# The mLSTM's values formed by feature in three jobs and turned by TensorE, the first beside the gates' columns; the last head's output gate copied out one key chunk sooner

## The reference, cut to what matters

```python
pf, mq, mk, mv, mo, mg, cq, ckv, kr = split_proj(h @ w_in[l])
...
v = heads(mv)                       # 4 heads x 96, as it is projected
g = (mg + b_g).reshape(...)         # 4 gates x 4 heads
...
s = jnp.einsum("bhtd,bhsd->bhts", qb, kb) * w_intra
num = jnp.einsum("bhts,bhsv->bhtv", s, vb) + w_inter[..., None] * jnp.einsum("bhtd,bhdv->bhtv", qb, C)
...
h = h.reshape(B, N, M_WIDTH) * g_m * jax.nn.sigmoid(mo)     # mo is the output gate
```

## Time and profile before

| | us |
|---|---|
| median of 3 runs | 3708.64 |
| lowest and highest | 3708.56, 3713.67 |
| the profiled execution | 3702.44 |
| its span, first to last instruction | 3700.6 |

### The profile page before, as it was taken

The page is one execution under the profiler, slowest core; times in us unless marked ns, Lnnn a source line. Parts: engine busy times, 40 slices in busy tenths (PEclk is TensorE's granted clock), DMA queues, the critical chain, the costliest instruction groups (busy, mean ns, idle before and its releaser), DMA issues.

```text
span 3700.6 us, 45082 instructions
## 1 busy us (share of the span) xinstructions
PE 3493.6 (94%) x17188; PEld 2741.7 (74%) x17188; DVE 2112.1 (57%) x2805; ACT 1190.5 (32%) x1448; POOL 246.5 (7%) x278
## 2 busy tenths in 40 slices
PE   7998998999998998999996999989998999999999
PEld 3786867888886776678885477778886567777887
DVE  6456547656657465566666555256666565354443
ACT  2235433122113255332223333332222343333222
POOL 0000100001000001000000000001100000000000
PEclk9999999999999999999998999999999999999999
DMA  8221202322321222034441021225443111222222
GB/s 338 81 76 52 72 1 92 114 102 91 125 102 64 78 75 78 15 138 169 160 159 59 24 75 48 89 91 194 159 159 114 49 52 57 80 99 84 101 92 102
DMA packets 52539, 361.67 MB, mean 98 GB/s; under 512 B 5992, under 2 KB 6632, under 8 KB 11056
## 3 DMA queue, kind: packets, MB, share of 16 engines
q1 hardware_dynamic: 36032, 259.01, 19.7%
q10 hardware_dynamic: 16368, 100.73, 7.4%
HBM read 357.40 MB, written 2.32 MB: 97 GB/s over the span
## 4 chain that ended last, share of the span: by engine, by line
PE 64%; issue 19%; DVE 11%; ACT 4%; DMA 0%; POOL 0%; DVEq 0%; POOLq 0%; ACTq 0%
PE pair L506 29%; PE pair L946 10%; PE pair L518 3%; PE pair L527 3%; PE pair L640 3%; PE pair L1019 2%; PE pair L539 2%; DVE arena L1987 2%; DVE w_lo L1927 1%; PE pair L868 1%; ACT w_hi L1306 1%; DVE x L1943 1%; PE pair L779 1%; PE pair L1089 1%; PE pair L843 1%
## 5 line engine op out<-in xcount | busy, mean ns | idle before, releaser
L1927 DVE TENSOR_TENSOR w_lo<-raw,w_hi 128x2048 fp32r<-128x2048 f32 x223 | 510.9, 2291 | 252.3 <-ACT w_hi L1306 246.6
L1306 ACT ACTIVATE w_hi<-raw 128x2048 fp32r<-128x2048 f32 x223 | 425.3, 1907 | 635.5 <-PE pair L506 579.7
L506 PE MATMUL pair<-h_hi,w_hi 128*128 128x512 f32 (+2 forms) x1760 | 576.2, 367 | 4.6 <-DVEq L1909 2.7
L506 PE MATMUL pair<-h_hi,w_lo 128*128 128x512 f32 (+2 forms) x1760 | 574.4, 366 | 0.0
L506 PE MATMUL pair<-h_lo,w_hi 128*128 128x512 f32 (+2 forms) x1760 | 572.8, 365 | 0.0
L506 PE MATMUL pair<-u_hi,w_hi 128*128 128x512 f32 (+3 forms) x1152 | 382.8, 368 | 12.6 <-DVE x L1943 5.9
L506 PE MATMUL pair<-u_hi,w_lo 128*128 128x512 f32 (+3 forms) x1152 | 382.0, 368 | 0.0
L1987 DVE SCALAR_TENSOR_TENSOR arena<-arena,cact 128x256 f32<-128x256 f32 x756 | 370.6, 513 | 19.5
L506 PE MATMUL pair<-u_lo,w_hi 128*128 128x512 f32 (+3 forms) x1152 | 381.2, 367 | 0.0
L2091 DVE TENSOR_TENSOR u_lo<-arena,u_hi 128x512 fp32r<-128x512 f32 (+1 forms) x128 | 97.1, 759 | 469.9 <-POOL arena L2584 452.5
L1943 DVE SCALAR_TENSOR_TENSOR x<-pair,mod,x 128x512 f32<-128x512 f32 (+1 forms) x408 | 267.5, 688 | 159.1 <-PE pair L506 136.1
(11 more groups left out here) (310 smaller groups left out, 4948.9 us busy)
## 6 DMA issues: line engine op xcount, KB each, us to landing
raw<-in_wt_dram SPq DMA_DIRECT2D x224, 1024.0 KB, 4.8
arena<-in_modw_dram ACTq DMA_DIRECT2D x78, 1024.0 KB, 5.0
arena<-in_modw_dram SPq DMA_DIRECT2D x18, 1024.0 KB, 7.1
arena<-negm_rows_dram ACTq DMA_DIRECT2D x16, 384.0 KB, 4.3
arena<-in_fconst_dram ACTq DMA_DIRECT2D x2, 2688.0 KB, 9.2
x<-in_xt_dram SPq DMA_DIRECT2D x1, 3072.0 KB, 16.4
arena<-in_brope_dram ACTq DMA_DIRECT2D x4, 640.0 KB, 3.9
out_dram<-x SPq DMA_DIRECT2D x1, 2048.0 KB, 7.2
```

The costliest lines, as they stand in the source:

```text
L506: mm = pe.matmul(pp[p][0:m, lo:hi], a[0:rows, k * width + c0:k * width + c0 + m], b[0:rows, k, lo:hi], start=(k == 0 and i == 0), stop=(k ...
L1306: act.activation(w_hi[slot][:], raw[slot][:], ACT.Copy).then_inc(w_hi_done, 1)
L1927: dve.tensor_tensor(w_lo[slot][:], raw[slot][:], w_hi[slot][:].bitcast(F32), ALU.subtract)\
```

## The change

On TensorE, the gates' 100 columns and the first 128 of the 384 value columns share one weight tile and make two feature jobs (pairs 0 and 1); the other 256 value columns are one tile and two feature jobs (pairs 2 and 3). The six token jobs are gone, and one weight tile a layer with them. ScalarE copies each value job to SBUF (`v_f`, three areas where the decays lie later), TensorE turns them with 18 transposes of 128x128 into pairs 2, 3 and 0 after the gates' 12 small transposes, and ScalarE copies these three into `va`. In the last head `og` is copied after the decays of j = 0. VectorE's third `split()` of the gates' stage is gone, and in the last head the second `split()` stands after `normalise` instead of after j = 3.

```diff
@@ tensor, mlstm
-                feature_job(w, KC, P, 0, 100, 100, H, T_ALL, 0, tile_used)
-                for v in range(2):
-                    w = tile()
-                    for i in range(3):
-                        toks = [(a * 192, slice((2 * i + a) * P, (2 * i + a + 1) * P)) for a in range(2)]
-                        token_job(w, 0, 192, 192, toks, 1 - (3 * v + i) % 2, tile_used if i == 2 else job_act)
+                feature_job(w, KC, P, 0, 100, 228, H, T_ALL, 0, job_act)
+                feature_job(w, KC, P, 100, P, 228, H, T_ALL, 1, tile_used)
+                w = tile()
+                feature_job(w, KC, P, 0, P, 256, H, T_ALL, 2, job_act)
+                feature_job(w, KC, P, P, P, 256, H, T_ALL, 3, tile_used)
...
+                pair_read(3)
+                for i, p in enumerate((2, 3, 0)):
+                    take_pair(p)
+                    for a in range(2):
+                        for c in range(3):
+                            at = 384 * a + P * c
+                            mm = pe.transpose(pp[p][:, at:at + P], v_f[c][:, (2 * i + a) * P:(2 * i + a + 1) * P], ident[:])
+                    mm.then_inc(job_act, 1)
                 barrier()
@@ scalar, mlstm
-                job(last=True)
+                job()
...
-                for v in range(2):
-                    split()
-                    for i in range(3):
-                        p = 1 - (3 * v + i) % 2
-                        job(last=i == 2)
-                        src = pp[p][:, 0:384].rearrange("p (a b c) -> p a b c", a=2, c=MD)
-                        act.activation(va[:, 2 * i:2 * i + 2, 2 * v:2 * v + 2, 0:MD], src, ACT.Copy)\
-                           .then_inc(pair_free[p], 1)
+                job(last=True)
+                act.activation(v_f[0], pp[1][:, 0:T_ALL], ACT.Copy).then_inc(pair_free[1], 1)
+                split()
+                for c in range(1, 3):
+                    job(last=c == 2)
+                    act.activation(v_f[c], pp[c + 1][:, 0:T_ALL], ACT.Copy).then_inc(pair_free[c + 1], 1)
...
+                for i, p in enumerate((2, 3, 0)):
+                    job()
+                    src = pp[p][:, 0:T_ALL].rearrange("p (a b c) -> p a b c", a=2, c=MD)
+                    act.activation(va[:, 2 * i:2 * i + 2, :, 0:MD], src, ACT.Copy).then_inc(pair_free[p], 1)
                 barrier()
...
-                        if j == 1:
+                        if j == (1 if h + 1 < MH else 0):
@@ vector, mlstm
                 ins.then_inc(dve_pe, 1)
-                split()
                 job()
...
-                        if j in ((2,) if h < MH - 1 else (1, 3)):
+                        if j == (2 if h < MH - 1 else 1):
                             split()
 
                 dve.wait_ge(pv_done, t.now(pv_done, 2))
                 normalise(MH - 1)
+                split()
                 heard()
                 output(MH - 1)
```

More of the change, by code:

```diff
@@ L258, in program @@
         W0 = D0 + 4 * T_ALL
+        v_f = [area(D0 + c * T_ALL, T_ALL) for c in range(3)]
         wgt = [[area(W0 + (d * 2 + i) * T_ALL, T_ALL) for i in range(2)] for d in range(2)]
@@ L531, in _ @@
             U, H = (u_hi, u_lo), (h_hi, h_lo)
[L533 to L541, removed]
             def folded_products(tiles, i, s, sums, vectors):
@@ L2702, in _weights @@
                 g[:, 64 * i + 32 * d:64 * i + 32 * d + 4] = w[:, g0 + 8 * d + 4 * i:g0 + 8 * d + 4 * i + 4]
-        tiles.append(_w_tile(g))
-        for v in range(2):
-            tiles.append(_w_tile(w[:, v0 + 192 * v:v0 + 192 * (v + 1)]))
+        tiles.append(_w_tile(np.concatenate([g, w[:, v0:v0 + 128]], 1)))
+        tiles.append(_w_tile(w[:, v0 + 128:v0 + 384]))
         qk = [_w_tile(np.concatenate([w[:, b + MD * h:b + MD * (h + 1)] for b in (q0, k0)], 1)) for h in range(MH)]
```

## The result

The changed kernel takes 3684.03 us (median of four runs, 3682.50 to 3687.90) beside 3708.60 us for the kernel before (four runs, 3699.66 to 3713.67). The ratio on record is 0.9947, with a 95% interval of 0.9932 to 0.9962: faster beyond the noise by 19.6 us, though by less than 2%. How this ratio weighs the single runs isn't on record; the quotient of the means is 0.9938 (23.0 us). The profiled execution took 3687.90 us with a span of 3685.5.

A forecast was written before the change was run, and what follows sets the result against it. TensorE, busy 94% of the span, was taken as the bound. 2 x 4.4 (stage) + 1.3 + 1.75 (last heads) = 11.9 us off 3708.64 gave 3696.7 us, range 3689 to 3706.

The forecast's parts named there:

- The level: Last step of the sum: the runs' median lay 6.2 us above the profiled execution, kept as a difference, giving 3696.7 us.
- The stage: Gates' stage, first gates' matmul to head 0's projection: 6.7 us gained on products, tail 4.60 instead of 2.27, 4.4 us a layer.
- The delay on VectorE: Gates' running sums on VectorE come 2.2 us later; 2.1 us of cover is left, so it costs nothing.
- rival 3: Gates' chain late on VectorE, delay over 4.3 us: TensorE waits; at 1 us beyond, 3698.7 us; chance 0.04.
- The last head: Earlier `og` copy gives 1.3 us in each layer; the moved `split()` ends a 0.45 us wait in the second, making 1.75.
- so all of it moves: First layer's last head: TensorE is busy without a gap from 369.3 to 387.3, so the path shortens by the full 1.3 us.
- rival 2: The last head gives nothing, as the full clock may come back no sooner; 8.8 us left, 3699.8 us; chance 0.12.
- The split now behind `normalise`: Last head: it stands under the `cq` product and costs nothing; had TensorE to wait, up to 2.29 us a layer.
- I take no fall: Gates' stage tail: the clock stays up through the new 4.60 us pause, with some 3.2 us of work in it.
- Rival 1: The clock falls behind the stage's transposes in one or both layers, 1.6 to 3.3 us each: 3698 to 3703; chance 0.30.
- a full clock sooner in the last heads: Lower end of the range: full clock back sooner in the two last heads, 3 to 4 us more gained.

## Why the prediction was wrong

**The level, 6.2 us.** The step that failed by most is the last one of the sum, a size and not a mechanism: "The median of the runs lies 6.2 us above it; I keep the difference". The three runs of 3708.56 to 3713.67 were taken as the kernel's level. Over all 117 runs the kernel before has a mean of 3702.5 (3689.09 to 3715.45, standard deviation 5.9), and its profiled execution, 3702.44, stood on it; the 21 runs of the changed kernel have 3684.1 (3677.32 to 3691.23). That the profiled execution stood on the mean is luck. From 3702.44 the same sum gives 3690.5. The spread "of one kernel (3708.56 to 3713.67)", 5 us, was likewise that of three runs; it is 26.

**The stage, right.** 4.4 us a layer were forecast, 4.74 and 4.72 came. The 96 pairs took 33.88 us against 8.55 + 25.44 = 33.99. The tail took 4.36 instead of 4.60: the copies are 0.74 us each, where 0.81 was taken from a single one, and six transposes take 0.89 us with the last one's latency, so ScalarE sets the pace as forecast.

**The delay on VectorE, right.** 2.2 us of cover left, 2.1 forecast; rival 3 did not occur.

**The last head, right in the waits and not in "so all of it moves".** The waits lost 1.28 us against 1.3, and 1.27 + 0.45 = 1.72 against 1.75. The path behind them moved by what the clock made of it: in the first pair of profiles by 1.6 and 0.7 us. Over three profiles of each kernel the paths are on average 1.9 and 2.4 us shorter (33.0 to 31.1, 28.4 to 25.9), 4.3 us for 3.0 of waiting. So rival 2, by which nothing is gained, did not occur, but its reason, that the full clock may come back no sooner, is what took 1.0 us in the second layer of the first pair. The split now behind `normalise` cost nothing.

**The clock at the stage, a term left out.** "I take no fall" held, in 12 of 12 stages. What was missed is that the old tail did fall, in 9 of 16; the one profile of the kernel before happened to have neither. Rival 1, with 0.30, asked only whether the new stage would lose something and not whether the old one did. Worth 1.9 us by the estimate above.

**The clock elsewhere, about 4 us, not forecast.** By means over all runs the change is worth 3702.5 − 3684.1 = 18.4 us (19.6 by the first ratio; 16.7, 19.7 and 23.0 on single chips). The waits and the stage are 12.5, the falls at the stage 1.9; some 4 are left. The prediction put the clock into the sum as nothing and into the rivals as a loss; only its range allowed 3 to 4 us for a full clock sooner in the last heads, and 1.3 us of the 4 is there (4.3 for 3.0). The 16 us less at 1.2 GHz come to 5.8 us, the whole of 1.9 and 4, and the gain stays when 8.5 and 17 us of work are put ahead. How the stage does it is open. The size is uncertain too: taken run by run the error of the difference is 1.1 us, but eight groups of runs of the kernel before have means from 3699.8 to 3709.5 and three of the changed kernel 3681.4 to 3685.4, by which it is nearer 2.

In sum: 6.2 from the level, 0.6 from the steps, 1.9 and about 4 from the clock make the 12.7 us between 3696.7 and 3684.0.

## What to carry to other kernels

Check the level before the sum: with three runs, the profiled execution and the median are two draws of one spread, and a forecast should take something between them and a range of the whole spread. When TensorE must wait several us between dense products, put its transposes there: 18 of them kept the clock up here where 3 did not, and one profile without a fall doesn't say that the old code has none. Count a gain in the path behind a wait and not only in the wait, for the clock can take part of it or add to it. Of two forms of a product with the same columns, the one with more columns for each load of the array was faster here (0.58 ns a column for steps of 192, 0.46 for 512 and 256 by turns, 0.45 for 384), and one that needs no turning afterwards gave a shorter tail too.

## What the runs showed of the hardware

Transposes kept the clock at 2.4 GHz through a pause of 4.36 us in 12 of 12 stages, where three of them instead of 18 let it fall in 4 of 4. Six fp32 transposes of 128 x 128 took 0.89 us, and all 18 took 2.19 us in the second layer, about 0.12 us each with the last one's latency in it. The same code, 857 us in the kernel before, took one of a few times in eighteen profiles: 848.8, 850.0 to 850.1, 850.8 to 850.9, 852.2, 853.0 to 853.1, or 856.7 to 856.9 us. The same kernel gave 848.8, 850.1 and 853.0 in three executions, so a single profile doesn't tell which of them a change brings. Single executions of the kernel before spread over 26 us, and those with less time at 1.2 GHz were the shorter ones (0.37 us for each us).
